# Encoder trunk on one core: one gate group ahead of the last state-space outputs, the GELU product among the score sums, the first norm's scaling on VectorE

## The chip, the cores and the metric

The program runs on one core of a Trainium2 chip. A core has four compute engines that run side by side, each with its own instruction queue: TensorE (matmuls and transposes, PE in the profile), VectorE (DVE), ScalarE (ACT) and GpSimd (POOL). SyncE (SP) has a queue too and issues most transfers. They wait for each other through semaphores. The time is the device time of one execution in microseconds, as the median of several runs. All tensors are float32.

## The reference, cut to what matters

256 tokens of width 1024 pass through one layer: a norm, a trunk with chunked attention and a state-space branch, a second norm, 32 experts of which each token takes four, and a third norm.

```python
h = layer_norm(x, ln_in_g, ln_in_b)
proj = h @ w_in                      # q, k, v, u: 512 columns each; gate logits: 2048
gates = sigmoid(gate_logits + b_gate)
y_attn = chunked_rel_attention(q, k, v, rel_bias) @ w_up_attn
y_s = s5_ssm(u, ...)                 # a scan over time in 32 groups, then outputs
glu_a, glu_b = split(gelu(y_s) @ w_glu)
y_ssm = (glu_a * sigmoid(glu_b)) @ w_up_ssm
mix = (g_attn * y_attn + g_ssm * y_ssm) @ w_o
h = layer_norm(ALPHA * h + mix, ln1_g, ln1_b)
h = layer_norm(ALPHA * h + moe_ffn(h, ...), ln2_g, ln2_b)
```

The norm divides by the deviation and then applies a gain and a shift per column. The kernel uses the normed rows twice: transposed for the projections, where gain and shift are applied on the way out of PSUM, and as rows `h` for the residual `ALPHA * h + mix`, where gain and shift need a pass of their own over 128 x 2 x 1024 elements. That pass is what is called the first norm's scaling here.

## The kernel before

Nothing schedules this program: each engine's instructions are written out in its own function, in the order in which the engine runs them, with the waits between them.

**Trunk, TensorE.** After 16 transposes, the projection with `w_in` is done in groups. A group is one 128-column slice of the output for all 256 tokens: 8 matmuls of 128x256, all on line L967 (`project`), into one of two PSUM banks in turn. So group g may start only once group g - 2 has been read. Groups 0 to 15 are u, q, k and v, groups 16 to 31 the 2048 gate columns. They are written between the state-space steps: `inputs_of_states` (L991) and `outputs_of_states` (L1005), four blocks b each. Before the change groups up to 27 are done when `outputs_of_states(3)` comes; it waits for VectorE's last states (L713) and for `y_used`, the read of block 2's outputs (L719). Then come the attention scores (L1038: first those of query tile a = 1 into banks 2 to 5, then of a = 0 into banks 6 and 7), gate groups 28 to 31, the GLU matmuls (L1059, 32 of them, into banks 4 and 5 and then 2 and 3), the up-projection of the state-space branch (groups 32 to 39, 4 matmuls each), the transposes of the softmax (L1077 to L1082), attention times V (L1093, L1094), the up-projection of attention (groups 40 to 47) and the output projection (L1111), then the transposes of the second norm (L1119) and the router.

**VectorE.** It does the state scan of each block, reads the outputs of block b (`y_block`, L719), builds the argument of the GELU in `gel` (L734 to L736), adds bias to the scores in twelve pieces (L753: a = 1 first, with chunks c = 0 and c = 1 of four pieces each, then a = 0), takes maxima (L756, L757), multiplies `uT` with the sigmoid that ScalarE made (L760, the GELU product, signal `gelu_ready`), normalizes the softmax (L762), does the GLU product (L771) and the gated sums: L780 for the state-space branch; for attention L799 (PSUM times gate into `gel`) and L801 (`mixT` plus `gel`, both in SBUF) for each of eight groups. L809 is the first residual.

**ScalarE.** It reads the groups 0 to 31 out of PSUM (`evac`, L385 and L391 for the gates), makes the sigmoid of the GELU (L408) after group 27, the exponentials (L417) and the GLU's sigmoids (L421).

**GpSimd.** After the softmax's transposes (`pt_psum` 6) it issues the transfer of the first norm's gain and shift rows into `rows` (which is `mid`, free by then), and of the experts' output biases; it waits for the rows and does the first norm's scaling: L531 (times gain) and L532 (plus shift), each one instruction over all of `h`, then the signal `h_ready`. After that it waits for the second norm's rows (`ln1_in`) and takes the power for its deviation (L485).

**SyncE.** Weights stream in through a ring of four blocks for the trunk, and the expert weights go into `gu_ring` and `dn_ring` as their parts come free. Its queue is strictly in order: behind the loads of expert 0's second matrix (L259) it waits for `h_ready`, loads the second norm's rows (L274) into the same `rows`, and then goes on with ten 1 MB loads of expert weights, each pair behind its own wait.

**Experts.** 16 pairs of experts, one loop iteration each: first matrix (L1220), bias (L1229), activation on ScalarE and VectorE, transposes (L1252), second matrix (L1259), combination into the sums (L1206). Each load of the next expert's weights waits until TensorE has used the part that it overwrites.

Of the kernel before, what the change touches and what calls it, by code (L numbers as in the profile page):

```python
# [10 lines left out]
ALU = mybir.AluOpType  # L11
# [39 lines left out]
def trunk_and_moe(nc, x, w_in, w_glu, w_ua, w_us, w_o, w_gu, w_dn, rel_bias, router_w, router_b,  # L51
                  cols_d, bc_d, consts_d, lnrows_d, bgu_d, bdn_d, out):
    with ExitStack() as ctx:
# [173 lines left out]
        def _(sp):  # L227
# [44 lines left out]
            sp.wait_ge(h_ready, 1)  # L272
            for r in range(2):
                sp.dma_start(rows[:, r, :], lnrows_d[2 + r:3 + r, :].to_broadcast([P, D])).then_inc(ln1_in, 16)  # L274
# [8 lines left out]
            load_gu(1, 1, 7)  # L283
            sp.wait_ge(wo_done, 3)
# [56 lines left out]
        def _(act):  # L341
# [63 lines left out]
            for g in range(G_GATE + 4, G_GATE + 12):  # L405
                evac(g)
            act.wait_ge(gelu_arg, 1)
            act.activation(gel, gel, ACT.Sigmoid, scale=2.0 * GELU_C).then_inc(gelu_sig, 1)  # L408
            for g in range(G_GATE + 12, G_US):
                evac(g)  # L410
# [60 lines left out]
        def _(pool):  # L471
# [58 lines left out]
            pool.wait_ge(lnin_in, 32)  # L530
            link(pool.tensor_tensor(h[:, :, :], h[:, :, :], rows[:, 0, :].unsqueeze(1).to_broadcast([P, TT, D]), ALU.mult))  # L531
            pool.tensor_tensor(h[:, :, :], h[:, :, :], rows[:, 1, :].unsqueeze(1).to_broadcast([P, TT, D]), ALU.add).then_inc(h_ready, 1)  # L532
# [43 lines left out]
        def _(dve):  # L576
# [165 lines left out]
            for a, Sx in ((1, S1), (0, S0)):  # L742
                for c in range(2):
                    nk = CHUNK * (2 * a + c + 1)
                    q = slice(64 * c, 64 * c + 64)
                    rev = slice(nk - 1, None, -1)
                    for half in range(2 * (a + 1)):
                        dve.wait_ge(score_psum, half // 2 + 1 if a else 3)
                        hs = 2 if a else 4
                        hh = slice(4 * (half // 2) + half % 2, 4 * (half // 2) + half % 2 + 2 * hs - 1, 2)  # L750
                        src = ps[2 + half] if a else ps[6 + half]
                        src = src[q, :].rearrange("p (h k) -> p h k", h=hs)[:, :, 0:nk]
                        dve.tensor_tensor(Sx[q, hh, 0:nk], src, relb[q, hh, rev], ALU.add).then_inc(score_used, 1)  # L753
# [5 lines left out]
            dve.wait_ge(gelu_sig, 1)  # L759
            dve.tensor_tensor(uT, uT, gel, ALU.mult).then_inc(gelu_ready, 1)  # L760
# [43 lines left out]
            dve.wait_ge(h_ready, 1)  # L804
# [134 lines left out]
        def _(pe):  # L939
# [91 lines left out]
            from_h(G_GATE + 8, 6, [0, 1, 2, 3])  # L1031
            outputs_of_states(3)
# [17 lines left out]
            from_h(G_GATE + 12, 7)  # L1050
# [4 lines left out]
            pe.wait_ge(gelu_ready, 1)  # L1055
            for bank, c0 in ((4, AW), (2, 0)):
# [269 lines left out]
```

## Time and profile before

| | us |
|---|---|
| median of 3 runs | 1210.28 |
| lowest and highest | 1208.54, 1211.18 |
| span of the profiled execution, first to last instruction | 1207.1 |
| TensorE busy in it | 1146.2 |
| VectorE, ScalarE, GpSimd busy in it | 307.6, 157.3, 61.3 |

The profiled execution comes with its span alone; what lies around a span is in the times of the runs and not in it. Busy shares say who works, not who is waited for: TensorE works nearly all of the span. So the chain that ended last, and the waits of TensorE, are the views to start with, and the timelines of the other engines in the stretch where TensorE waits. The trunk ends at about 234 us of the span, the rest is experts and the last norm. The profile counts each float32 matmul and each weight load as two instructions, so that a group of 8 matmuls stands as x16.

### The profile page before, as it was taken

Reading aid. Unit: us, or ns where it says so; the run is one execution under the profiler, and the core shown is the slowest. Engines: PE = TensorE matmul, PEld = TensorE weight load, DVE = VectorE, ACT = ScalarE, POOL = GpSimd, SP = SyncE. Lnnn points to the kernel's source line nnn. Section 1 sums busy time; section 2 is a strip of 40 time slices with the busy share of each in tenths; the row PEclk is TensorE's granted clock in tenths of the full one; section 3 lists DMA queues with packets and bytes.
Section 4 is the critical chain, followed back from the end, with each engine's and each line's share of the span. In section 5 each row is a group of like instructions: output and inputs, shape, how many; then the busy total and the mean of one; then the engine's idle time right before and its main releaser. Section 6 shows DMA issues by size and latency. Waiting matters only on the chain.

```text
span 1207.1 us, 13899 instructions
## 1 busy us (share of the span) xinstructions
PE 1146.2 (95%) x5396; PEld 538.7 (45%) x5396; DVE 307.6 (25%) x586; ACT 157.3 (13%) x293; POOL 61.3 (5%) x82
## 2 busy tenths in 40 slices
PE   6999999899999999999999999999999999999996
PEld 5788885533333333333333333333333333333332
DVE  5899653511111111111111111111111111111114
ACT  4222400111010101010101010101010101010100
POOL 4000040300000000000000000000000000000000
PEclk9999999999999999999999999999999999999998
DMA  9643876499999999999999999999999996999990
GB/s 347 187 139 132 328 256 260 185 366 419 418 417 418 418 418 417 418 418 417 418 417 418 418 417 418 418 418 418 418 418 418 417 418 241 385 417 416 418 378 36
DMA packets 88855, 438.06 MB, mean 363 GB/s; under 512 B 8224, under 2 KB 9376, under 8 KB 56064
## 3 DMA queue, kind: packets, MB, share of 16 engines
q1 hardware_dynamic: 87840, 435.14, 89.4%
q0 software_dynamic: 704, 2.49, 0.7%
q8 instruction: 15, 0.25, 0.1%
q10 hardware_dynamic: 288, 0.12, 0.0%
q14 instruction: 8, 0.07, 0.0%
HBM read 436.67 MB, written 1.05 MB: 363 GB/s over the span
## 4 chain that ended last, share of the span: by engine, by line
PE 84%; DVE 12%; ACT 2%; issue 1%; DMA 0%; SPq 0%; DVEq 0%; POOL 0%
PE ps L1220 37%; PE ps L1259 19%; PE ps L1206 9%; PE ps L967 5%; PE ps L1229 5%; PE ps L1157 3%; PE ps L1111 2%; ACT mid L453 2%; PE ps L1252 1%; DVE mid L698 1%; PE ps L1059 1%; DVE wide L910 1%; DVE wide L913 1%; DVE wide L906 1%; DVE mid L688 1%
## 5 line engine op out<-in xcount | busy, mean ns | idle before, releaser
L1220 PE MATMUL ps<-gu_ring,hT_mem 128*64 128x512 f32 x2048 | 445.8, 593 | 0.0
L1220 PEld LDWEIGHTS ps<-gu_ring,hT_mem 128*64 128x64 f32 x2048 | 148.1, 137 | 292.2 <-issue 292.1
L1259 PE MATMUL ps<-dn_ring,mid 128*64 128x512 f32 x1024 | 226.8, 595 | 24.3 <-ACT mid L453 24.3
L906 DVE TENSOR_SCALAR wide<-ps 128x512 f32<-128x512 f32 x32 | 22.1, 691 | 515.2 <-PE ps L1229 515.2
L1259 PEld LDWEIGHTS ps<-dn_ring,mid 128*64 128x64 f32 x1024 | 73.0, 137 | 157.6 <-issue 155.7
L1206 PE MATMUL ps<-mid,attnT 128*128 128x512 f32 x256 | 115.2, 593 | 0.0
L445 ACT ACTIVATE wide<-wide 128x512 f32<-128x512 f32 x32 | 20.2, 630 | 643.9 <-DVE wide L906 643.9
L967 PE MATMUL ps<-hT_mem,gu_ring 128*128 128x256 f32 x448 | 99.6, 382 | 0.0
L915 DVE COPY mid<-ps 128x512 f32<-128x512 f32 x32 | 22.1, 691 | 289.4 <-PE ps L1259 289.4
L967 PEld LDWEIGHTS ps<-hT_mem,gu_ring 128*128 128x128 f32 x448 | 84.2, 190 | 14.2 <-issue 2.1
L1157 PEld LDWEIGHTS ps<-Pm,h 128*128 128x128 f32 x544 | 65.1, 196 | 13.5 <-issue 13.5
L1157 PE MATMUL ps<-Pm,h 128*128 128x128 f32 x544 | 69.8, 283 | 0.0
L1206 PEld LDWEIGHTS ps<-mid,attnT 128*128 128x128 f32 x256 | 46.2, 191 | 45.9 <-issue 45.9
L550 POOL TENSOR_TENSOR wide<-consts,ones 128x256 f32<-128x256 f32 x32 | 19.8, 620 | 847.0 <-PE ps L1229 844.9
L1229 PE MATMUL ps<-mid,wide 128*64 128x512 f32 x256 | 60.5, 593 | 0.0
L1229 PEld LDWEIGHTS ps<-mid,wide 128*64 128x64 f32 x256 | 18.6, 137 | 35.8 <-issue 35.8
L1252 PE MATMUL ps<-consts,wide 128*128 128x128 f32 x128 | 20.1, 279 | 11.3 <-DVE wide L913 11.3
L456 ACT ACTIVATE hT_mem<-ps 128x512 f32<-128x512 f32 x16 | 9.6, 597 | 147.7 <-PE ps L1157 147.7
L1111 PE MATMUL ps<-gu_ring,hT_mem 128*128 128x512 f32 x64 | 28.3, 595 | 0.0
L453 ACT ACTIVATE mid<-ps 128x512 f32<-128x512 f32 x32 | 19.1, 597 | 52.1 <-PE ps L1252 52.1
L1252 PEld LDWEIGHTS ps<-consts,wide 128*128 128x128 f32 x128 | 14.7, 140 | 22.6 <-DVE wide L913 14.2
L910 DVE SCALAR_TENSOR_TENSOR wide<-wide 128x512 f32<-128x512 f32 x32 | 22.1, 692 | 3.3
(197 smaller groups left out, 614.6 us busy)
## 6 DMA issues: line engine op xcount, KB each, us to landing
gu_ring<-in_w_gu_dram SPq DMA_DIRECT2D x256, 1024.0 KB, 14.1
dn_ring<-in_w_dn_dram SPq DMA_DIRECT2D x128, 1024.0 KB, 11.5
gu_ring<-in_w_in_dram SPq DMA_DIRECT2D x16, 1024.0 KB, 9.9
gu_ring<-in_w_o_dram SPq DMA_DIRECT2D x4, 1024.0 KB, 6.2
gu_ring<-in_w_glu_dram SPq DMA_DIRECT2D x2, 1024.0 KB, 5.9
gu_ring<-in_w_us_dram SPq DMA_DIRECT2D x2, 1024.0 KB, 5.9
gu_ring<-in_w_ua_dram SPq DMA_DIRECT2D x2, 1024.0 KB, 6.7
mid<-in_lnrows_dram POOLq DMA_DIRECT2D x3, 512.0 KB, 5.2
```

The costliest lines, as they stand in the source:

```text
L453: act.activation(actT[:, :, :].rearrange("p k c -> p (k c)"), psY[:, :], ACT.Copy).then_inc(at_ready, 1)
L906: dve.tensor_scalar(xg, psA[:, :], LIMIT, None, ALU.min).then_inc(xg_ready, 1)
L910: dve.scalar_tensor_tensor(out=xl, in0=xl, scalar=1.0, in1=xg, op0=ALU.add, op1=ALU.mult).then_inc(lin_ready, 1)
L915: dve.tensor_copy(ysb, psY[:, :]).then_inc(y_ready, 1)
L967: ins = pe.matmul(bank_of(g), lhs(k), rhs(k), start=(k == 0), stop=(k == nk - 1))
L1111: ins = pe.matmul(ps[4 + 2 * tt + hf][:, :], mixT[:, k, tt * P:(tt + 1) * P], wo[:, k, :], start=(k == 0), stop=(k == KD - 1))
L1157: ins = pe.matmul(bank[:, (k % 4) * P:(k % 4) * P + P], h[:, tt, k * P:(k + 1) * P], Pm[:, tt, :], start=(tt == 0 and k % 4 == 0), stop=(t ...
L1206: pe.matmul(ps[2 * tt + hf][:, :], GTz[:, a, hf, tt * P:(tt + 1) * P], ysb, start=False, stop=False, skip_group_check=True).then_inc(combi ...
L1220: ins = pe.matmul(bank[64 * hf:64 * hf + 64, :], XT[:, k, CAP * a:CAP * a + CAP], gu_ring[:, a, k, q * 512:(q + 1) * 512], start=(i == 0), ...
L1229: ins = pe.matmul(bank[64 * hf:64 * hf + 64, :], sel4[a][:, q, :], bgu, start=False, stop=True, skip_group_check=True)
L1252: ins = pe.transpose(psY[:, j * P:(j + 1) * P], xl[:, j * P:(j + 1) * P], ident)
L1259: ins = pe.matmul(psY[64 * hf:64 * hf + 64, :], actT[:, k % 4, CAP * (k // 4):CAP * (k // 4) + CAP], dn_ring[:, k, hf * 512:(hf + 1) * 512 ...
```

## The change

Three things move. On TensorE group 28, the first of the last four gate groups, is put before `outputs_of_states(3)`, and ScalarE reads it before it makes the GELU's sigmoid. On VectorE the GELU product moves from behind the maxima to a place between the eight score additions of a = 1, after the first four; since `gelu_ready` no longer tells that banks 2 to 5 have been read, TensorE waits for `score_used` 8 before the GLU matmuls. The first norm's scaling leaves GpSimd and is done by VectorE after the eight attention sums, in four instructions of 128x1024 instead of two of 128x2048; the load of the second norm's rows, which waits for it, moves behind six loads of expert weights in SyncE's queue.

```diff
--- before.py
+++ after.py
@@ -269,9 +269,6 @@
             sp.wait_ge(pv_psum, 2)
             for j in J_ORDER:
                 load_dn(0, j)
-            sp.wait_ge(h_ready, 1)
-            for r in range(2):
-                sp.dma_start(rows[:, r, :], lnrows_d[2 + r:3 + r, :].to_broadcast([P, D])).then_inc(ln1_in, 16)
             sp.wait_ge(proj_done, G_UA)
             load_gu(0, 0, 2)
             load_gu(0, 0, 3)
@@ -281,6 +278,9 @@
             sp.wait_ge(mix_ready, KD)
             load_gu(1, 1, 6)
             load_gu(1, 1, 7)
+            sp.wait_ge(h_ready, 1)
+            for r in range(2):
+                sp.dma_start(rows[:, r, :], lnrows_d[2 + r:3 + r, :].to_broadcast([P, D])).then_inc(ln1_in, 16)
             sp.wait_ge(wo_done, 3)
             load_gu(0, 0, 6)
             load_gu(0, 0, 7)
@@ -402,11 +402,11 @@
             for g in range(G_V, G_GATE + 4):
                 evac(g)
             tables(3)
-            for g in range(G_GATE + 4, G_GATE + 12):
+            for g in range(G_GATE + 4, G_GATE + 13):
                 evac(g)
             act.wait_ge(gelu_arg, 1)
             act.activation(gel, gel, ACT.Sigmoid, scale=2.0 * GELU_C).then_inc(gelu_sig, 1)
-            for g in range(G_GATE + 12, G_US):
+            for g in range(G_GATE + 13, G_US):
                 evac(g)
 
 
@@ -527,9 +527,6 @@
             pool.memset(bdn[2 * E:P, :], 0.0).then_inc(bdn_zero, 1)
             pool.dma_start(bdn[0:E, :], bdn_d).then_inc(bdn_in, 16)
             pool.wait_ge(bdn_zero, 2)
-            pool.wait_ge(lnin_in, 32)
-            link(pool.tensor_tensor(h[:, :, :], h[:, :, :], rows[:, 0, :].unsqueeze(1).to_broadcast([P, TT, D]), ALU.mult))
-            pool.tensor_tensor(h[:, :, :], h[:, :, :], rows[:, 1, :].unsqueeze(1).to_broadcast([P, TT, D]), ALU.add).then_inc(h_ready, 1)
             pool.wait_ge(ln1_in, 32)
             for tt in range(TT):
                 inverse_deviation(tt)
@@ -744,6 +741,9 @@
                     nk = CHUNK * (2 * a + c + 1)
                     q = slice(64 * c, 64 * c + 64)
                     rev = slice(nk - 1, None, -1)
+                    if a == 1 and c == 1:
+                        dve.wait_ge(gelu_sig, 1)
+                        dve.tensor_tensor(uT, uT, gel, ALU.mult).then_inc(gelu_ready, 1)
                     for half in range(2 * (a + 1)):
                         dve.wait_ge(score_psum, half // 2 + 1 if a else 3)
                         hs = 2 if a else 4
@@ -756,8 +756,6 @@
                 link(dve.tensor_reduce(negmax[:, a, :], Sx, AX_X, ALU.max))
             dve.tensor_scalar(negmax[:, :, :], negmax[:, :, :], -1.0, None, ALU.mult).then_inc(max_ready, 1)
 
-            dve.wait_ge(gelu_sig, 1)
-            dve.tensor_tensor(uT, uT, gel, ALU.mult).then_inc(gelu_ready, 1)
             def normalize(a, Sx):
                 dve.tensor_tensor(Sx, Sx, psums[:, a, :].unsqueeze(2).to_broadcast([P, HEADS, P * (a + 1)]), ALU.mult).then_inc(p_norm, 1)
 
@@ -801,7 +799,11 @@
                 dve.tensor_tensor(mixT[:, n, :], mixT[:, n, :], gel[:, n % 2, :], ALU.add).then_inc(mix_ready, 1)
 
 
-            dve.wait_ge(h_ready, 1)
+            dve.wait_ge(lnin_in, 32)
+            for tt in range(TT):
+                link(dve.tensor_tensor(h[:, tt, :], h[:, tt, :], rows[:, 0, :], ALU.mult))
+                link(dve.tensor_tensor(h[:, tt, :], h[:, tt, :], rows[:, 1, :], ALU.add))
+            dve.sem_inc(h_ready, 1)
 
             def residual(tt, i):
 
@@ -1029,6 +1031,7 @@
             from_h(G_GATE + 4, 5, [1, 2, 3])
             outputs_of_states(2)
             from_h(G_GATE + 8, 6, [0, 1, 2, 3])
+            from_h(G_GATE + 12, 7, [0])
             outputs_of_states(3)
 
 
@@ -1047,12 +1050,13 @@
             for hd in range(HEADS):
                 ins = score(hd, slice(0, P), P, ps[6 + hd % 2][:, hd // 2 * P:hd // 2 * P + P])
             ins.then_inc(score_psum, 1)
-            from_h(G_GATE + 12, 7)
+            from_h(G_GATE + 12, 7, [1, 2, 3])
 
 
             wg = stream[B_GLU % 4].rearrange("p (k n) -> p k n", k=KA)
             pe.wait_ge(*w_there(B_GLU))
             pe.wait_ge(gelu_ready, 1)
+            pe.wait_ge(score_used, 8)
             for bank, c0 in ((4, AW), (2, 0)):
                 for i in range(4):
                     for k in range(KA):
```

On TensorE, around the last state-space outputs (L1005 before, L1007 in the changed program), before:

```order
L1005 MATMUL ps<-wide,dn_ring 32x256 x8
L967 MATMUL ps<-hT_mem,gu_ring 128x256 x32
L1005 MATMUL ps<-wide,dn_ring 32x256 x8
L1038 MATMUL ps<-dn_ring 128x256 x8
L1038 MATMUL ps<-dn_ring 128x128 x8
L967 MATMUL ps<-hT_mem,gu_ring 128x256 x32
L1059 MATMUL ps<-dn_ring,gu_ring 128x256 x32
```

and in the changed program:

```order
L1007 MATMUL ps<-wide,dn_ring 32x256 x8
L969 MATMUL ps<-hT_mem,gu_ring 128x256 x40
L1007 MATMUL ps<-wide,dn_ring 32x256 x8
L1041 MATMUL ps<-dn_ring 128x256 x8
L1041 MATMUL ps<-dn_ring 128x128 x8
L969 MATMUL ps<-hT_mem,gu_ring 128x256 x24
L1063 MATMUL ps<-dn_ring,gu_ring 128x256 x32
```

One group, eight matmuls, stands before the outputs instead of behind the scores.

On VectorE, from the GELU's argument to the normalization of the softmax, before:

```order
L734 TENSOR_TENSOR wide<-dn_ring 128x1024
L735 TENSOR_SCALAR wide<-wide 128x1024
L736 TENSOR_TENSOR wide<-wide,dn_ring 128x1024
L740 MEMSET mid 64x8x64
L741 MEMSET mid 64x8x64
L753 TENSOR_TENSOR mid<-ps,dn_ring 64x2x192 x4
L753 TENSOR_TENSOR mid<-ps,dn_ring 64x2x256 x4
L753 TENSOR_TENSOR mid<-ps,dn_ring 64x4x64 x2
L753 TENSOR_TENSOR mid<-ps,dn_ring 64x4x128 x2
L756 TENSOR_REDUCE negmax<-mid 128x8 x2
L757 TENSOR_SCALAR negmax<-negmax 128x16
L760 TENSOR_TENSOR dn_ring<-dn_ring,wide 128x1024
```

and in the changed program, where the GELU product is L746:

```order
L737 MEMSET mid 64x8x64
L738 MEMSET mid 64x8x64
L753 TENSOR_TENSOR mid<-ps,dn_ring 64x2x192 x4
L746 TENSOR_TENSOR dn_ring<-dn_ring,wide 128x1024
L753 TENSOR_TENSOR mid<-ps,dn_ring 64x2x256 x4
L753 TENSOR_TENSOR mid<-ps,dn_ring 64x4x64 x2
L753 TENSOR_TENSOR mid<-ps,dn_ring 64x4x128 x2
L756 TENSOR_REDUCE negmax<-mid 128x8 x2
L757 TENSOR_SCALAR negmax<-negmax 128x16
```

The product moved ahead of eight additions, the maxima and their negation.

On SyncE, after the loads of the output projection's weights; one piece of the difference, in which L283 is the load of the second norm's rows:

```order
 L259 DMA dn_ring<-in_w_dn_dram 128x2x1024 x4
-L274 DMA mid<-in_lnrows_dram 128x1024 x2
-L256 DMA gu_ring<-in_w_gu_dram 128x2048 x10
+L256 DMA gu_ring<-in_w_gu_dram 128x2048 x6
+L283 DMA mid<-in_lnrows_dram 128x1024 x2
+L256 DMA gu_ring<-in_w_gu_dram 128x2048 x4
```

Six expert loads passed the two loads of rows.

## Rows read from the trace of the kernel before

**Rows 1.** The page: the span, and the chain that ended last by engine

```profile
span 1207.1 us, 13899 instructions
...
PE 84%; DVE 12%; ACT 2%; issue 1%; DMA 0%; SPq 0%; DVEq 0%; POOL 0%
```

**Rows 2.** Waits of TensorE, 119 to 235 us: for whom, us, times, longest

```profile
PE ps L1005 <- DVE dn_ring L719: 2.6, 1, 2.6
PE ps L1170 <- DVE attnT L834: 1.6, 1, 1.6
PE ps L1119 <- DVE h L616: 1.4, 1, 1.4
PE ps L967 <- DVE wide L799: 1.2, 1, 1.2
```

**Rows 3.** Waits of TensorE, 234 to 1190 us

```profile
PE ps L1259 <- ACT mid L453: 24.3, 32, 0.8
```

**Rows 4.** The chain that ended last, in order of time: start, length, what

```profile
122.37 1.07 PE ps L1005 x16
...
126.26 14.01 PE ps L967 x64
140.27 13.89 PE ps L1059 x64
...
209.69 0.87 PE ps L1119 x8
```

**Rows 5.** Timeline of ScalarE, 127 to 152 us: start, length, instruction, idle before

```profile
127.26 1.06 ACT L408 ACTIVATE wide<-wide 128x1024 f32<-128x1024 f32 x1 [6.99 <-DVE wide L736]
...
140.80 1.28 ACT L417 ACT_TABLE_LOAD   x1
142.09 0.40 ACT L417 ACTIVATE mid<-mid,negmax 128x128 f32<-128x128 f32 x1
...
150.52 1.09 ACT L421 ACTIVATE wide<-ps 128x512 f32<-128x512 f32 x2
```

**Rows 6.** Timeline of VectorE, 128 to 155 us

```profile
128.44 6.61 DVE L753 TENSOR_TENSOR mid<-ps,dn_ring 64x384 f32<-64x384 f32 x12
...
138.74 1.22 DVE L760 TENSOR_TENSOR dn_ring<-dn_ring,wide 128x1024 f32<-128x1024 f32 x1
...
154.26 0.69 DVE L771 TENSOR_TENSOR wide<-ps,wide 128x512 f32<-128x512 f32 x1 [2.42 <-PE ps L1059]
```

**Rows 7.** Timeline of GpSimd, 175 to 206 us

```profile
175.01 4.51 POOL L532 TENSOR_TENSOR h<-h,mid 128x2048 f32<-128x2048 f32 x1
204.85 0.57 POOL L485 TENSOR_TENSOR rstd<-mv,half_power 128x1 f32<-128x1 f32 x1 [25.33 <-DVE mv L596]
```

**Rows 8.** Timeline of VectorE, 175 to 228 us

```profile
175.61 0.42 DVE L799 TENSOR_TENSOR wide<-ps,gu_ring 128x256 f32<-128x256 f32 x1 [1.30 <-PE ps L967]
176.07 3.73 DVE L801 TENSOR_TENSOR hT_mem<-hT_mem,wide 128x256 f32<-128x256 f32 x1
...
182.22 0.42 DVE L799 TENSOR_TENSOR wide<-ps,gu_ring 128x256 f32<-128x256 f32 x1 [0.83 <-PE ps L967]
...
189.59 0.43 DVE L801 TENSOR_TENSOR hT_mem<-hT_mem,wide 128x256 f32<-128x256 f32 x1
196.07 0.69 DVE L809 SCALAR_TENSOR_TENSOR h<-h,ps 128x512 f32<-128x512 f32 x1 [6.06 <-PE ps L1111]
...
205.46 1.00 DVE L616 TENSOR_SCALAR h<-h,mv,rstd 128x512 f32<-128x512 f32 x2 [0.75 <-POOL rstd L485]
...
226.15 1.64 DVE L865 TENSOR_TENSOR h<-h,mid 128x512 f32<-128x512 f32 x1
```

**Rows 9.** Stretches: us, busy PE, PEld, DVE, ACT, POOL, PEclk, DMA share, GB/s

```profile
176.00:178.00 2.00, 2.00 (x11) 1.74 (x10) 1.97 (x2) 0.00 (x0) 2.00 (x1) 1.00 1.02 418
```

**Rows 10.** The page's transfers: what, count, KB each, median us to landing

```profile
mid<-in_lnrows_dram SPq DMA_DIRECT2D x2, 512.0 KB, 6.0
```

**Rows 11.** Stretches, the one before the first expert, columns as in rows 9

```profile
230.80:234.30 3.50, 3.50 (x18) 3.50 (x18) 2.64 (x16) 0.60 (x1) 1.19 (x2) 0.51 0.01 2
```

## The prediction

> **What bounds the kernel now.** I read the page first, then the chain of work that ended last, then the waits of TensorE in the one stretch that the change touches. The span is 1207.1 us and 84% of the chain is TensorE's [rows 1]. So only TensorE's idle time or TensorE's work can give time back, and the change takes away no matmul: it has as many before and after. What is left is idle time between 119 and 235 us. There the waits name four pieces; the change is aimed at two of them, 2.6 us before the last state-space outputs (L1005) and 1.2 us among the attention up-projections (L967, held by VectorE's L799) [rows 2]. Behind the trunk the expert loop shows TensorE held only by short ScalarE and VectorE handoffs, 0.8 us at the longest, and never by a transfer [rows 3]. Each load there is released by TensorE's own progress, so a trunk that ends earlier moves the whole loop earlier by as much, and I add nothing and take nothing away for it.
>
> **First part, the gate group ahead of the last outputs.** L1005 starts at 122.37 and TensorE waited 2.6 us for that, so the group before it ended at 119.8 [rows 2, 4]. Of the next four gate groups, 14.01 us in the chain, one takes 14.01 / 4 = 3.5 us [rows 4]. Put ahead, it fills the 2.6 us and runs on to 123.3, so the outputs start 0.9 us later than now. From L1005's start to the end of the scores is 126.26 - 122.37 = 3.9 us, so to 127.2; three groups of 3.5 follow, to 137.7, where the four end now at 126.26 + 14.01 = 140.27. TensorE is **2.6 us** early at the GLU matmuls (L1059), if it may start them.
>
> It may if the GELU product is there and the score banks are read. The last y block is 0.9 us later, and all VectorE does after it. The score additions (L753) then start at 128.44 + 0.9 = 129.3. All twelve take 6.61 us, 0.55 each, so the first four end at 131.5. The sigmoid on ScalarE starts at 127.26 + 0.9 = 128.2 and lasts 1.06, to 129.2: the product in its new place does not wait. It takes 1.22 us (L760), to 132.7, and the second four additions, 2.2 us at the mean and 2.8 at most (they are the wide ones), end by 134.9 to 135.5 [rows 5, 6]. The new wait for eight score reads thus ends 2.2 us or more before TensorE comes at 137.7. In the old place the product would have ended at 138.74 + 0.9 + 1.22 = 140.9, so the gate group alone would have won nothing: the move is what pays it out.
>
> What the move costs: the maxima end at about 138.8 (the product behind them starts at 138.74), and then at 138.8 + 0.9 + 1.2 = 140.9. ScalarE cannot use them earlier now anyway, since its last gate read is followed by a 1.28 us table load, and the exponentials start at 142.09. Then the last gate read ends about 138.2, the table is there at 139.5, and they start at 140.9: 1.2 us earlier than now, while TensorE is 2.6 earlier, so the softmax loses 1.4 us of cover. What covers it is TensorE's GLU, 13.9 us: VectorE's second GLU product (L771) waits 2.42 us for TensorE now, at 154.26. In the changed kernel ScalarE's two GLU sigmoids end at 150.52 + 1.09 - 1.2 = 150.4 and TensorE at 137.7 + 13.9 = 151.6. TensorE is still last, by 1.2 us, and from there all goes on 2.6 us earlier [rows 5, 6]. Next in line, if more were shifted, is that 1.2.
>
> **Second part, the first norm's scaling.** POOL's two passes over h run until 175.01 + 4.51 = 179.52 [rows 7]. VectorE's first L801, an addition with both operands in SBUF, starts at 176.07 and lasts 3.73 us, up to 179.80, where the later ones take 0.42; L799, which reads PSUM, is not stretched [rows 8]. So I read the 3.73 as VectorE held until POOL ended. TensorE has two banks, so it ran two more groups before it stopped: L799 of group 0 starts at 175.61, one of these groups, half as deep as a gate group, takes 3.5 / 2 = 1.75 us, so group 3 should have been read at 175.61 + 3 x 1.75 = 180.9, and was at 182.22 [rows 8]. The loss is **1.4 us**; its lower bound is the 1.2 of the wait [rows 2], its upper bound the stretch itself, 3.73 - 0.42 = 3.3, which the two banks exclude. Without POOL's passes it is gone, and the pair L799, L801 (0.9 us) fits in 1.75.
>
> The Trainium skill has a rule for this place: "SBUF — State Buffer", section "SBUF: two separate sides", says that VectorE and GpSimd share one pair of ports, and that a VectorE operation with two SBUF inputs is held for the whole of a GpSimd operation that reads SBUF. This trace agrees with it (3.73 against 0.42 us). The same rule speaks against the change too, since the four new VectorE operations have two SBUF inputs each; it bites only if POOL works beside them.
>
> The four new operations are 128x1024 with both inputs in SBUF, as L760 is (1.22 us) [rows 6]; each waits for the one before, some 0.04 us, so 5.0 us. They stand after the last L801, which now ends at 190.0, and before L809, ahead of which VectorE idles 6.06 us for TensorE's first output projection [rows 8]. **Cost 0**, with 1.0 us to spare; beyond that each us costs one, as TensorE waits for the residual soon after. The scaling rows must have landed before POOL's first pass, which ends ahead of 175.01 [rows 7], so VectorE doesn't wait for them.
>
> **Third part, SyncE's queue.** Four loads of expert 0's weights (the pairs behind 40 and 48 groups) no longer stand behind the scaling; nothing waits for them before the expert loop, more than 40 us later, so 0. The rows of the second norm move the other way: now issued at about 179.5, when POOL is done; then when VectorE is done, 190.0 - 4.0 + 5.0 = 191, and behind four 1 MB loads released from 185.1 on. At 418 GB/s [rows 9] one takes 2.5 us, so the four end at 195.1 and the two row loads, 1 MB in all, at 197.7; with their whole 6.0 us to landing [rows 10] put on top instead, 201.1. POOL waits for these rows before its first power (L485), 204.85 now, 200.8 then [rows 7]. What TensorE sees is later: it reaches the transposes at 209.69, and the half of h that it wants is ready at about 205.46 + 0.56 = 206.0 [rows 4, 8], 3.7 us before. So the rows would have to land after 200.8 + 3.7 = 204.5 to cost anything. I take 0; the later bound of 201.1 costs 0 too.
>
> **The sum.** 2.6 + 1.4 = 4.0 us. The profiled span becomes 1207.1 - 4.0 = 1203.1; the median of the runs, 1210.28, lies 3.2 us above that span, which I leave as it is: **1206.3 us**, 0.33% less.
>
> One term is left that no edit sets. From 230.8 to 234.3 TensorE's granted clock is 0.51, its lower level of 1.2 GHz instead of 2.4, after idle pieces of 1.4 and 1.6 us shortly before [rows 2, 11]. That is 3.5 us of work at half speed, so 1.7 us lost. The idle pieces before it stay, but whether the fall comes, and how much dense work it meets, may differ: 1.7 us either way. The three runs of before lie 2.6 us apart, which is of that size.
>
> **Rivals.**
> A. *The stall is not POOL's.* Then L801 keeps its 3.7 us and only the first part counts: 1210.28 - 2.6 = 1207.7. For it: one instance only. Against it: it ends 0.3 us after POOL's pass, and its seven sisters are short. 8%.
> B. *The softmax chain takes over.* If the additions, the maxima or the exponentials run over 1.2 us later than summed, TensorE waits at the GLU or at the transposes and gives the 2.6 back: 1210.28 - 1.4 = 1208.9. For it: the smallest cover that I lean on. Against: all terms are measured durations in unchanged order. 8%.
> C. *VectorE's scaling is stretched (the other side).* Beside POOL, L865 takes 1.64 us for 128x512 [rows 8]; twice that, 3.3 for 128x1024, four times, is 13.1, less the 6.06 idle: 7.0 us on the path, 1210.28 - 4.0 + 7.0 = 1213.3. It turns the sign from 6.06 + 4.0 = 10.1 us for the four, 2.5 each. Against: POOL then only waits for the rows, with nothing to read. 4%.
> D. *The row loads land late.* From 204.5 on it costs one for one; the gain is gone at 208.5, some 11 us after my sum. Near 1209 to 1212. 4%.
> E. *The clock.* The fall is missing (1204.6) or comes twice or over denser work (1208.0). 10%, half each.
>
> **How the numbers follow.** The forecast, 66%, has 1205.0 to 1207.7 for its own range (smaller clock shifts and the spread of three runs). About 0.2%, 2.4 us, is what a measurement here can tell from no change: faster means below 1207.9. Faster: 63 of the 66, 6 of A's 8, 1 of B, 6 of E's 10: 76%. Slower (above 1212.7): most of C and a little of D, 5%. The rest, 19%, is no difference. To hold 8 in 10 the range takes in A and E's ends and B: 1204.0 to 1209.0.
>
> **What the changed profile would show.** TensorE's wait at the last state outputs gone, ScalarE's thirteenth gate read before the GELU sigmoid; the GLU matmuls starting near 137.7 with no wait; exponentials from about 140.9; every L801 sister at 0.42; four operations of about 1.23 us after them and some 1 us of VectorE idle before the first residual; POOL's power not later than 201; the expert loop 4 us earlier with its period unchanged. I am wrong if TensorE waits before the GLU or the transposes, if POOL waits for a transfer past 204, or if the loop takes the 4 us back.

## The result

The changed kernel takes 1204.97 us in the median (1203.12 to 1206.93, 4 runs), the kernel before 1210.73 us beside it (1208.54 to 1211.33, 4 runs): ratio 0.9956, 95% interval 0.9939 to 0.9973. That is 5.3 us by the ratio, with 3.3 to 7.4 inside the interval; 4.0 had been forecast, as 1206.3 us, and the time lies in the range of 1204.0 to 1209.0.

### The profile page after: what moved, and what is told of

Same layout as the page of the kernel before. It is cut to its first block, busy times and chain, and to the rows that moved or that the text cites. A ratio compares the mean times of both kernels' runs of the same rounds, so it can differ in the third digit from the quotient of the medians.

```text
span 1205.0 us, 13900 instructions
## 1 busy us (share of the span) xinstructions
PE 1148.1 (95%) x5396; PEld 540.6 (45%) x5396; DVE 309.8 (26%) x590; ACT 157.3 (13%) x293; POOL 52.3 (4%) x80
## 4 chain that ended last, share of the span: by engine, by line
PE 92%; DVE 5%; ACT 2%; issue 1%; DMA 0%; SPq 0%; DVEq 0%; POOL 0%
PE ps L1224 37%; PE ps L1263 19%; PE ps L969 12%; PE ps L1210 9%; PE ps L1233 5%; PE ps L1161 3%; PE ps L1115 2%; ACT mid L453 2%; PE ps L1256 1%; PE ps L1063 1%; DVE wide L912 1%; DVE wide L915 1%; DVE wide L908 1%; DVE wide L909 1%; PE ps L1243 1%
```

## The profile after

The page of the changed kernel: the span (1207.1 before, rows 1), and TensorE's busy time, which is not smaller.

```profile
span 1205.0 us, 13900 instructions
...
PE 1148.1 (95%) x5396; PEld 540.6 (45%) x5396; DVE 309.8 (26%) x590; ACT 157.3 (13%) x293; POOL 52.3 (4%) x80
```

The waits of TensorE, 119 to 235 us, to be held beside [rows 2]: for whom, us in total, times, longest. The two waits that the change was aimed at are gone; the two before the first expert, for the second norm's rows (L1123) and for the router (L1174), are as they were.

```profile
PE ps L1174 <- DVE attnT L836: 1.7, 1, 1.7
PE ps L1123 <- DVE h L613: 1.4, 1, 1.4
```

The chain that ended last, to be held beside [rows 4]: start, length, what. TensorE now goes without a break from the gate groups through the last outputs (L1007), the scores, three gate groups and the GLU (L1063), and the last two up-projections of the state-space branch and the eight attention groups are one piece of 17.46 us, where before VectorE's addition of 3.73 us stood between pieces of 5.39 and 8.90.

```profile
123.74 1.00 PE ps L1007 x16
124.74 2.82 PE ps L1041 x32
127.56 10.56 PE ps L969 x48
138.12 13.81 PE ps L1063 x64
...
167.97 17.46 PE ps L969 x80
185.44 20.60 PE ps L1115 x48
```

VectorE's timeline, to be held beside [rows 6, 8]. The product (L746) stands between the additions; the second GLU product (L769) still waits for TensorE, 0.99 us; the first addition of the attention sums (L799 here) takes 0.42 instead of 3.73; the four scaling operations take 1.22 to 1.23 each, and 1.07 us of idle time is left in front of the first residual.

```profile
131.62 1.20 DVE L746 TENSOR_TENSOR dn_ring<-dn_ring,wide 128x1024 f32<-128x1024 f32 x1
132.86 4.62 DVE L753 TENSOR_TENSOR mid<-ps,dn_ring 64x512 f32<-64x512 f32 x8
...
152.04 0.69 DVE L769 TENSOR_TENSOR wide<-ps,wide 128x512 f32<-128x512 f32 x1 [0.99 <-PE ps L1063]
...
173.85 0.42 DVE L799 TENSOR_TENSOR hT_mem<-hT_mem,wide 128x256 f32<-128x256 f32 x1
...
186.27 1.22 DVE L804 TENSOR_TENSOR h<-h,mid 128x1024 f32<-128x1024 f32 x1
187.53 1.23 DVE L805 TENSOR_TENSOR h<-h,mid 128x1024 f32<-128x1024 f32 x1
188.79 1.23 DVE L804 TENSOR_TENSOR h<-h,mid 128x1024 f32<-128x1024 f32 x1
190.05 1.23 DVE L805 TENSOR_TENSOR h<-h,mid 128x1024 f32<-128x1024 f32 x1
192.34 0.69 DVE L811 SCALAR_TENSOR_TENSOR h<-h,ps 128x512 f32<-128x512 f32 x1 [1.07 <-PE ps L1115]
```

So both steps are there as forecast. But the profiled span is only 2.1 us shorter. One reason is the head: ScalarE reads group 27 at 120.33 instead of 119.80, 0.5 us later, ahead of everything that the change touches. The other is the clock. The stretch in front of the first expert, to be held beside [rows 11] (us, busy PE, PEld, DVE, ACT, POOL, granted clock, DMA share, GB/s), is at half clock for 7.0 us here, and was for 3.5 before:

```profile
225.20:232.20 7.00, 6.45 (x24) 5.42 (x24) 3.63 (x22) 0.84 (x3) 1.33 (x3) 0.52 0.12 37
```

To see past both I cut every profile at the same events: A, from ScalarE's read of gate group 27 to the first GLU matmul; B, to the first attention up-projection; C, to the first output projection; D, to GpSimd's second power (L485); E, to the first expert matmul; F, to the end. The starts are those of the timelines, in which a first matmul begins up to 0.2 us before its place in the chain. The four rows that A and C are read from, before:

```profile
119.80 0.47 ACT L391 ACTIVATE gu_ring<-ps,cols 128x256 f32<-128x256 f32 x1 [2.98 <-PE ps L967]
140.10 14.05 PE L1059 MATMUL ps<-dn_ring,gu_ring 128*128 128x256 f32 x64
173.68 5.34 PE L967 MATMUL ps<-attnT,gu_ring 128*128 128x256 f32 x24
188.93 20.76 PE L1111 MATMUL ps<-gu_ring,hT_mem 128*128 128x512 f32 x48
```

and in the changed kernel:

```profile
120.33 0.47 ACT L391 ACTIVATE gu_ring<-ps,cols 128x256 f32<-128x256 f32 x1 [2.98 <-PE ps L969]
137.96 13.98 PE L1063 MATMUL ps<-dn_ring,gu_ring 128*128 128x256 f32 x64
171.46 13.98 PE L969 MATMUL ps<-attnT,gu_ring 128*128 128x256 f32 x64
185.27 20.76 PE L1115 MATMUL ps<-gu_ring,hT_mem 128*128 128x512 f32 x48
```

All stretches in us:

| kernel | A | B | C | D | E | F |
|---|---|---|---|---|---|---|
| before, first profile | 20.30 | 33.58 | 15.25 | 32.99 | 12.62 | 972.56 |
| before, second profile | 23.30 | 33.51 | 15.23 | 32.98 | 12.31 | 972.59 |
| changed, first | 17.63 | 33.50 | 13.81 | 32.99 | 14.15 | 972.59 |
| changed, second | 17.63 | 33.51 | 13.81 | 32.99 | 14.12 | 972.65 |
| changed, third | 17.63 | 33.50 | 13.82 | 32.99 | 13.96 | 972.61 |

B, D and F agree within 0.1 us. **A is 2.67 us shorter at equal clock, C 1.44: 4.1 us for the edits, against 4.0 in the sum.** What remains lies in A and E, and both are questions of the clock. The experiments take the parts one by one.

## Experiments

### The two parts of the first step

The gate group alone, with the product left in its place:

```diff
             from_h(G_GATE + 8, 6, [0, 1, 2, 3])
+            from_h(G_GATE + 12, 7, [0])
             outputs_of_states(3)
...
-            from_h(G_GATE + 12, 7)
+            from_h(G_GATE + 12, 7, [1, 2, 3])
```

> One part alone: gate group 28 ahead of the last state-space outputs, the GELU product still behind the maxima, the first norm's scaling still on GpSimd. My theory (the move of the product is what pays the group out): the product ends 0.9 us later than in the kernel before, at about 140.9 us, TensorE comes to the GLU at 137.7 and waits 3.2 us there; net 0.6 us slower than before (1.0005), with L967's 1.2 us wait on L799 unchanged. Rival (the group alone is worth its idle time): 2.6 us faster, 0.998, and no wait at the GLU. The clock's fall near 226 to 234 us adds noise of 1.7 to 3.5 us to single runs, so the verdict is read from the waits and from runs of equal mean clock.

Ratio 1.0012 (1.0001 to 1.0023), 12 runs, median 1212.46 against 1210.52. ScalarE reads group 28 before the GELU's sigmoid here too. TensorE's waits name the GLU, and its timeline shows what followed:

```profile
PE ps L1060 <- DVE dn_ring L760: 3.3, 1, 3.3
```

```profile
141.36 17.09 PE L1060 MATMUL ps<-dn_ring,gu_ring 128*128 128x256 f32 x64 [3.30 <-DVE dn_ring L760]
```

The wait is 3.3 us (3.2 expected) and A is 21.09, 0.8 longer than 20.30 (0.6 expected). The surprise is the GLU itself: 17.09 us instead of 14.05, since the clock is at its lower level from 140.7 to 147.5 us, from the end of this wait on. B is 36.62, 3.1 us longer. So without the product's move the gate group wins nothing in the median, and a wait of 3.3 us can cost as much again. The runs lie in two groups: four at a mean clock of 0.996 take 1208.6 to 1209.7 us, the other eight 1211.7 to 1215.2.

Both, with the scaling left on GpSimd:

```diff
+                    if a == 1 and c == 1:
+                        dve.wait_ge(gelu_sig, 1)
+                        dve.tensor_tensor(uT, uT, gel, ALU.mult).then_inc(gelu_ready, 1)
...
             pe.wait_ge(gelu_ready, 1)
+            pe.wait_ge(score_used, 8)
```

> Gate group 28 and the GELU product moved, the scaling left on GpSimd. Theory: the 2.6 us wait at the last state outputs is gone, no wait at the GLU, the 1.2 us wait on L799 behind GpSimd's passes stays: 2.6 us faster than before, 1.4 us slower than the changed kernel, at equal clock. Rival (the two parts are not additive, since an earlier TensorE meets GpSimd's passes otherwise): the stall among the attention sums grows or shrinks by more than 0.5 us.

Ratio 0.9961 (0.9949 to 0.9974). The median is 1205.90. A is 17.63, as in the changed kernel; C is 15.33, as before; E is 12.32. In A and C the two steps don't touch each other, and the step on TensorE and VectorE is worth its 2.67 us alone. That the total is as good as the changed kernel's is E: here the clock stayed full in front of the first expert.

### The scaling, and what holds VectorE

Only the scaling and the load of rows moved, as in the change:

```diff
-            link(pool.tensor_tensor(h[:, :, :], h[:, :, :], rows[:, 0, :].unsqueeze(1).to_broadcast([P, TT, D]), ALU.mult))
...
+            for tt in range(TT):
+                link(dve.tensor_tensor(h[:, tt, :], h[:, tt, :], rows[:, 0, :], ALU.mult))
+                link(dve.tensor_tensor(h[:, tt, :], h[:, tt, :], rows[:, 1, :], ALU.add))
```

> The scaling on VectorE and the moved load of rows alone, gate group and product as before. Theory: the first addition of the attention sums takes 0.42 us instead of 3.73, the wait on L799 is gone, 1.4 us faster than before at equal clock; the 2.6 us wait at L1005 stays. Rival (the stretch is not GpSimd's): that addition still takes 3 us or more and the time does not change.

Ratio 0.9992 (0.9983 to 1.0), median 1208.45 against 1210.52; the interval ends at "no change", so it is the profile that shows the step. C is 13.81, 1.44 less than before, the addition takes 0.42 us and the wait on L799 is gone. A shows something that the first profile of before did not: 21.90 instead of 20.30. TensorE's timeline there (start, length, instruction, idle before):

```profile
122.27 1.94 PE L1006 MATMUL ps<-wide,dn_ring 128*32 128x256 f32 x16 [2.60 <-DVE dn_ring L716]
124.14 3.62 PE L1039 MATMUL ps<-dn_ring 64*128 64x256 f32 x32
```

The state outputs take 1.94 us where the first profile of before has 1.07: the clock is at its lower level from 122.2 to 125.6 us, right behind the 2.6 us wait.

Is it GpSimd's reading that holds VectorE? The changed kernel with GpSimd multiplying `h` by ones twice where its scaling had stood:

```diff
+            pool.wait_ge(lnin_in, 32)
+            for _ in range(2):
+                ins = pool.tensor_tensor(h[:, :, :].rearrange("p a (b c) -> p (a b) c", c=P), h[:, :, :].rearrange("p a (b c) -> p (a b) c", c=P),
+                                         ones[:, :].unsqueeze(1).to_broadcast([P, TT * KD, P]), ALU.mult)
...
+            ins.then_inc(pool_held, 1)
...
             dve.wait_ge(lnin_in, 32)
+            dve.wait_ge(pool_held, 1)
```

> The changed kernel, with GpSimd multiplying h by ones in two passes of 128x2048 where its scaling stood before, VectorE's scaling waits for their end. Theory (VectorE's additions with two inputs in SBUF are held while GpSimd reads SBUF, whatever it computes): one of the eight L799 additions lasts 3.3 to 4.5 us, TensorE waits about 1.2 us again among the attention groups, 1.4 us slower than the changed kernel at equal clock, and VectorE's scaling, behind it, still takes 5.0 us. Rival (the stretch comes from the scaling's rows or transfers): no addition over 0.5 us.

VectorE's timeline, and GpSimd's beside it:

```profile
174.32 3.73 DVE L807 TENSOR_TENSOR hT_mem<-hT_mem,wide 128x256 f32<-128x256 f32 x1
```

```profile
168.66 9.12 POOL L533 TENSOR_TENSOR h<-h,ones 128x2048 f32<-128x2048 f32 x2 [2.40 <-DMA mid<-in_lnrows_dram]
```

The 3.73 us are back to the hundredth, and the addition ends at 178.0, 0.3 us after GpSimd. TensorE waits 1.2 us, C is 15.24. The needless passes cost in C the 1.43 us that the change had saved, with neither rows nor scaling in them. The time does not show it: median 1205.41, ratio 0.9960 (0.9944 to 0.9976), as the changed kernel. E is 12.31 here, since the clock did not fall in front of the first expert.

The same with GpSimd busy but not reading:

```diff
+            for _ in range(12):
+                link(pool.memset(bdn[2 * E:P, :], 0.0))
```

> The changed kernel, with GpSimd writing zeros over 64x1024 elements twelve times (0.95 us each, some 11 us in all) where its scaling stood before; it reads nothing from SBUF. Theory (only a GpSimd operation that reads SBUF holds VectorE's additions with two SBUF inputs): the L799 additions stay at 0.42 us, TensorE has no wait among the attention groups, time as the changed kernel. Rival (any GpSimd work on SBUF holds them): the first two or three of these additions last up to 1.0 us more each.

GpSimd's memsets run from 164.98 to 176.99; VectorE's additions at 173.06, 174.78 and 176.51 fall into that time and take 0.42 us each:

```profile
164.98 12.01 POOL L531 MEMSET mid<- 64x1024 f32 x12
```

```profile
173.06 0.42 DVE L801 TENSOR_TENSOR hT_mem<-hT_mem,wide 128x256 f32<-128x256 f32 x1
...
174.78 0.42 DVE L801 TENSOR_TENSOR hT_mem<-hT_mem,wide 128x256 f32<-128x256 f32 x1
...
176.51 0.42 DVE L801 TENSOR_TENSOR hT_mem<-hT_mem,wide 128x256 f32<-128x256 f32 x1
```

C is 13.81, the median 1205.86 (ratio 0.9961). So passes of GpSimd that read `h` hold the addition, and memsets do not. The memsets are also shorter (1.0 us against 4.5) and cover 64 partitions, so these runs alone do not single out the reading. The Trainium skill, "SBUF — State Buffer", section "SBUF: two separate sides", limits the lock for a VectorE operation with two SBUF inputs to GpSimd operations that read SBUF; these two runs agree with it, 3.73 against 0.42 us.

### How much cover the scaling has

The changed kernel with twice the work there:

```diff
                 link(dve.tensor_tensor(h[:, tt, :], h[:, tt, :], rows[:, 0, :], ALU.mult))
+                for _ in range(2):
+                    link(dve.tensor_tensor(h[:, tt, :].rearrange("p (b c) -> p b c", c=P), h[:, tt, :].rearrange("p (b c) -> p b c", c=P),
+                                           ones[:, :].unsqueeze(1).to_broadcast([P, KD, P]), ALU.mult))
```

> The changed kernel with four more VectorE operations of 128x1024 (a product with ones) among the four of the scaling, so that VectorE works 10.0 us there instead of 5.0. Theory (the scaling costs nothing because 6.06 us of VectorE's idle time cover it, and each us beyond is paid in full): the first residual 3.9 to 4.0 us later, TensorE waits that long less what its own queue still holds, the time up by 1 to 4 us against the changed kernel. I take 0.4 to 4: TensorE reaches the second norm's transposes 3.7 us after their operand is ready, so up to 3.7 us of the 4.0 may vanish there. If the transposes are what counts, the time goes up by only 0.3 us; if the first residual itself is waited for, by 4.0.

VectorE's timeline: the first residual starts at 196.37 instead of 192.34, and no longer waits for TensorE. The second one, 2 us on, still waits 1.32 us for TensorE:

```profile
196.37 0.69 DVE L814 SCALAR_TENSOR_TENSOR h<-h,ps 128x512 f32<-128x512 f32 x1 [0.17 <-DVE h L808]
...
199.10 0.69 DVE L814 SCALAR_TENSOR_TENSOR h<-h,ps 128x512 f32<-128x512 f32 x1 [1.32 <-PE ps L1118]
```

D is 32.99 and TensorE's waits are those of the changed kernel. The median is 1206.01; the changed kernel had 1205.61 beside it. 5 us more of VectorE's work cost nothing on the path. The first residual is not what TensorE waits for: behind it VectorE idles again for the second, and only what both delay reaches the norm. My lowest expectation, 0.3 us, was still too high for the path.

### The clock

The kernel before, for a second profile:

> The kernel before, unchanged, for a second profile. In the first one TensorE's clock fell once (230.8 to 234.3 us); the profile of the kernel with the scaling alone shows it falling at 121 to 125 us too, right behind the 2.6 us wait. Theory: the same can happen to the kernel before in some executions, and then L1005 and part of the scores take up to twice their time (1.5 us). Rival: in this kernel only the pieces before the first expert let the clock fall; then the granted clock at 119 to 130 us is 1.00 again.

The result decides for the first theory, though the fall lasted longer and cost twice what had been expected (3.0 us in A against 1.5). TensorE's timeline, and the stretches (columns as in rows 9):

```profile
121.33 1.93 PE L1005 MATMUL ps<-wide,dn_ring 128*32 128x256 f32 x16 [2.59 <-DVE dn_ring L719]
123.20 5.04 PE L1038 MATMUL ps<-dn_ring 64*128 64x256 f32 x32
```

```profile
121.20:128.20 7.00, 6.87 (x49) 4.87 (x49) 4.56 (x6) 1.06 (x1) 0.00 (x0) 0.54 1.02 421
226.00:234.00 8.00, 6.36 (x45) 5.21 (x45) 6.74 (x22) 1.90 (x6) 4.88 (x6) 1.00 0.39 163
```

Behind the 2.6 us wait TensorE works 7.0 us at the lower level; outputs and scores take 1.93 and 5.04 us instead of 1.07 and 2.89, and A is 23.30, 3.0 us more than in the first profile. In this execution the clock did not fall in front of the first expert. What the full clock gives there is little, because another wait shows up, which the first profile did not have:

```profile
PE ps L1220 <- ACT hT_mem L437: 1.2, 1, 1.2
```

E is 12.31 us at full clock and 12.62 with a fall of 3.5 us (rows 11). A fall of 7 us, as in all three profiles of the changed kernel, makes it 13.96 to 14.15.

The profiles also say how to read the mean clock of a run. Each of them ends with 5 to 7 us at the lower level, where TensorE has no work left. The five without any other fall have a mean clock of 0.997 or 0.998, the three of the changed kernel, with a 7 us fall besides, 0.994.

Does keeping TensorE busy in the first wait help by itself? The kernel before with needless matmuls in it:

```diff
+            pe.wait_ge(bu_used, 32)
+            for _ in range(11):
+                pe.matmul(ps[2][:, 0:P], ident, upper, start=True, stop=True, skip_group_check=True)
             outputs_of_states(3)
```

> The kernel before with 11 needless 128x128 matmuls (0.22 us each, 2.4 us in all) in TensorE's 2.6 us wait ahead of the last state-space outputs; no useful work moves. Theory (part of what the gate group is worth is that it keeps the clock up there): no fall at 120 to 130 us, 0.5 to 1.2 us faster than before in the median. Rival (filling the piece is worth only the work that is moved into it): same time as before, within 0.3 us.

Ratio 0.9993 (0.9984 to 1.0002), median 1209.16 against 1210.27. The profile has the full clock from 119 to 130 us and A at 20.29. The interval takes in "no change", so the times alone do not show the gain; but 5 of the 11 runs have a mean clock of 0.997 or 0.998, against 8 of 51 runs of the kernel before on the same chip, none of them at 0.998. The share saved is partly lost to a stall that was 0.7 us longer in this profile (C 15.94; the rows landed later, and with them GpSimd's passes).

Does it help in front of the first expert? The changed kernel with needless matmuls, 6 and 7, in both waits there, into spare columns of a bank:

```diff
+            def keep_busy(count):
+                for _ in range(count):
+                    pe.matmul(ps[6][:, 256:384], ident, upper, start=False, stop=True, skip_group_check=True)
...
             gather(0, psA, [0])
+            keep_busy(6)
             transpose_h1(1)
...
             gather(1, psM, [0])
+            keep_busy(7)
```

> The changed kernel with 6 and 7 needless 128x128 matmuls (0.22 us each) into an unused part of a PSUM bank, where TensorE waits 1.4 and 1.65 us before the first expert. Theory (what is left of the spread is the clock's fall there): no fall before the first expert, all runs in one group at the highest mean clock (0.998), the median 1 to 2 us below the changed kernel's. Rival (the fall there is hidden anyway, since at full clock TensorE waits 1.2 us for ScalarE's copy in front of the first expert): the clock is up but the median moves by under 0.5 us.

Ratio 0.9953 (0.9939 to 0.9967), median 1204.13, all 5 runs at a mean clock of 0.998. TensorE's timeline: the fill ends before the transposes need their operand, the waits of 1.4 and 1.6 us are gone from the list, and what is left is ScalarE's copy.

```profile
216.87 1.50 PE L1168 MATMUL ps<-consts 128*128 128x128 f32 x12
...
222.93 1.73 PE L1168 MATMUL ps<-consts 128*128 128x128 f32 x14
...
229.62 2.79 PE L1230 MATMUL ps<-gu_ring,hT_mem 128*64 128x512 f32 x12 [1.30 <-ACT hT_mem L437]
```

E is 12.37.

### The changed kernel again, and beside the filled one

> The changed kernel once more, beside the kernel before on the same chip. Theory: the edits are worth 4.0 us and what was measured beyond it (5.8 us between medians) is how often the clock falls before the first expert: runs of either kernel lie in groups about 1.7 us apart that differ in mean clock by 0.0014, and within a group the changed kernel is 4.0 us shorter (3.6 to 4.4). Rival (the edits themselves are worth 5.8): within a group of equal clock it is 5 us or more shorter.

Ratio 0.9961 (0.9948 to 0.9973), median 1205.63. The expectation of neat groups 1.7 us apart was wrong: four runs at 0.994 span 1203.3 to 1204.8 us, and the head of the kernel, before anything of this, varies by 1 us and more (group 27 is read at 118.7 to 120.8 us in the profiles). Mean clock does not sort the runs well enough to compare them in pairs; cutting the profiles at events does.

> The changed kernel once more, on one chip with the version that fills TensorE's waits. Theory: 4 to 5.5 us faster than before; from the GELU up to the GLU 17.8 us as in its other profiles, the clock full up to 220 us, and falling or not in front of the first expert: 12.3 us from GpSimd's second power to the first expert where it doesn't, up to 14.2 where it does. Rival (the clock may fall in the first part too): a stretch up to the GLU of 20 us or more.

> The changed kernel with 6 and 7 needless matmuls in TensorE's two waits before the first expert, once more, beside the changed kernel. Theory: 12.3 to 12.4 us from GpSimd's second power to the first expert, no fall of the clock in any run, 0.5 to 1.9 us faster than the changed kernel in the median. Rival: no difference beyond 0.3 us.

Changed: ratio to before 0.9954 (0.9940 to 0.9968), median 1205.61, mean clocks 0.994 three times, 0.997, 0.998. Changed and filled: 0.9946 (0.9932 to 0.9959), median 1203.70, all five at 0.998, E 12.34. On one chip the filled kernel is 1.9 us below the changed one, and 1.6 to 1.8 us come out of the profiles in E. On both chips it is the fastest kernel of this study. The intervals of the two ratios overlap; the profiles and the ten runs with one and the same clock are what speaks for it.

## Why the prediction came out

**The gate group** was forecast at 2.6 us and is 2.67 at equal clock (20.30 to 17.63). The steps under it held: no wait at the GLU; exponentials at 141.30, which less the 0.5 us of the head is 140.8 (140.9 forecast); 0.99 us of cover left at the second GLU product (1.2 forecast). That the product's move pays the group out was shown by leaving it away.

**The scaling** was forecast at 1.4 us and is 1.44. Rival A is out: the stall goes with GpSimd's reading and comes back with it.

**VectorE's four operations** took 5.0 us with 1.07 to spare (5.0 and 1.0 forecast) and cost nothing. The sentence behind it was wrong: "beyond that each us costs one". Another 5 us cost none, since VectorE idles again before the second residual. Rival C was therefore priced too high as well; its point of decision lies further out than the 10.1 us that I gave it, and at 10.0 us of work there is still no cost. (GpSimd read nothing beside these operations, so Rival C's own mechanism was not put to the test.)

**The rows of the second norm** landed late, as the upper bound had it. GpSimd's power, which waits for them, starts at 201.70, or 201.2 less the head's 0.5; 201.1 was the bound and 200.8 the need. The prediction's check "not later than 201" failed by this; TensorE saw none of it (D is unchanged), as its 3.7 us of slack said. The row (start, length, idle before):

```profile
201.70 0.57 POOL L485 TENSOR_TENSOR rstd<-mv,half_power 128x1 f32<-128x1 f32 x1 [35.92 <-DMA mid<-in_lnrows_dram]
```

**The clock** is the term that failed, in size and in place. The profiled span was forecast at 1203.1 and is 1205.0, of which 0.5 us is the head and 1.5 the clock in E. I had one fall in front of the first expert, costing 1.7 us for 3.5 us at half clock, "either way". There a fall of 3.5 us costs 0.3 us (12.62 against 12.31), because at full clock TensorE only waits for ScalarE's copy instead; a fall of 7 us costs 1.6 to 1.8. And the costliest fall of the kernel before, 3.0 us in A, stood in no row of the one profile of before: it comes behind the 2.6 us wait itself, in one of the two profiles of that kernel and in that of the scaling alone. Filling this wait with real work is thus worth 2.67 us at full clock and up to 3.0 more in the executions where the clock would have fallen; in all nine profiles of kernels with the group and the product moved, A is 17.62 or 17.63. Against that stands E: every profile of the changed kernel has the 7 us fall there, and by their mean clock of 0.994 nine of its 14 timed runs had it, the other five (0.997 and 0.998) not. From the mid-part of both (A to F without the head), the first profile of before has 1087.3 us, the second 1089.9, the three of the changed kernel 1084.5 to 1084.7: 2.6 to 5.4 us less, around the 4.1 of the edits. The ratios, 0.9954 to 0.9961 in three measurements, are 4.7 to 5.6 us; how much of what goes beyond 4.1 is the clock and how much the head's variation, the timed runs do not tell, as they have no timeline. That the median of 1204.97 is only 1.3 us from the forecast is in part luck: its four runs are two at 1203.1 and 1203.3 us with a mean clock of 0.998 and two at 1206.6 and 1206.9 with 0.994, and the median lies in the gap between them.

**What the times do not show** is the scaling's 1.4 us. It is in C of every profile, but the kernels that have the first step and a GpSimd pass beside the additions, with a median of 1205.90 (scaling left on GpSimd) and 1205.41 (needless passes), are as fast as the changed kernel with 1204.97 to 1205.63. The clock tells where it went. None of these nine runs has a mean clock under 0.996, and E is 12.32 and 12.31. Of the 21 runs of the three kernels without such a pass (the changed one, with memsets, with doubled scaling) 15 have 0.994, and in all five of their profiles the clock falls for 7 us in front of the first expert, with E at 13.87 to 14.15. So by these numbers the fall there, at 1.6 to 1.8 us, took back in most executions what the scaling had won. Where the clock stays up in both, the scaling is there in the times too: the filled kernel takes 1204.13 us, the one with the needless passes 1205.41 on the same chip at the same time.

What stays open: what decides whether, and for how long, the clock falls in front of the first expert. With the same waits of 1.4 and 1.6 us there it fell for 3.5 us (the first profile of before), for 7 us (the changed kernel, with memsets, with doubled scaling, and the gate group alone) or not at all (the second profile of before, the kernel before with its first wait filled, the scaling alone, gate group and product without the scaling, and the needless passes). That the fall came more often once the stall was gone is seen in the kernels that have the first step; no run shows why, and in the kernel with the scaling alone it did not come.

**The loop** moved as a whole (F 972.56 to 972.66 in all kernels), so nothing of a gain in the trunk is lost to its transfers.

## What to carry to other kernels

Work that is pulled into a wait pays only if the step that the engine comes to next has been pulled forward as well: the gate group alone won nothing (ratio 1.0012), group and product together gave 2.67 us. When a VectorE addition of two SBUF operands lasts as long as a neighbouring GpSimd pass, move the pass; moving it into an idle stretch of VectorE was free, with room for as much again. But look at the times too: here the 1.4 us that it won in its own stretch did not show in them, and the clock fell more often further on. And take more than one profile before you price a clock fall: cut them at the same events, and look for work at half clock behind every wait, here behind single ones of 2.6 and 3.3 us and behind 1.4 and 1.65 us in short order.

## What the runs showed of the hardware

- A VectorE tensor_tensor with two SBUF inputs was held until a GpSimd tensor_tensor on SBUF had ended (3.65 to 4.42 instead of 0.42 us, in all six profiles with such a pass), not by GpSimd memsets (0.42 us); operations with one operand in PSUM were not stretched (0.42 us beside GpSimd's pass).
- TensorE's clock fell from 2.4 to 1.2 GHz at the end of single waits of 2.6 and 3.3 us in otherwise dense stretches, and where waits of 1.4 and 1.65 us stood 5 us apart; it did so in some executions of a kernel and not in others. It stayed low for 3.5 or 7 us.
- Thirteen needless matmuls, 2.8 us of work in waits that were there anyway, kept the mean clock at 0.998 in ten of ten runs, where 3 of 14 runs of the same kernel without them had it and two more had 0.997.
- Two row loads of 0.5 MB behind four 1 MB loads of weights took 8.9 and 9.8 us to land, against 6.0 in the median when they stood ahead. Issued 5 us later, behind the doubled scaling, they took 4.0 and 4.9 us and landed no later, which points at the loads ahead of them.
